# Two transformer blocks on one core: four projection stages with the weights as the 512-column moving operand

## The reference

```
q, f, i, o_gate, pool_v, gate_a, gate_b = split(x @ w_in)
o = hgrn2(silu(q), 1 - f, i, log f)                    # 8 heads of 128
o = o * rsqrt(mean(o*o, per head) + eps)
o = o * norm_g * sigmoid(o_gate);  a = o @ w_a          # og
...
h = rmsnorm(x); q, k, v, gu, gv, ... = split(h @ w_in_2)
attention(rope(q), rope(k), v)                          # v2
z = spatial_gate(rmsnorm(gelu(gv)));  gelu(gu) * z      # gv
k, v = split(rmsnorm(mem) @ w_kv)                       # cross attention, xv
...
peer_ffn: top-16 of 128 x 128 expert keys per head, rows of w_down and w_up gathered
```

## Time and profile before

| what | value |
|---|---|
| median of 3 runs | 1317.92 us |
| profiled execution | 1317.83 us, its span 1315.7 us |
| busy share of the span | TensorE 91%, VectorE 70%, ScalarE 41%, GpSimd 21% |
| chain that ended last, by engine | TensorE 57%, DMA 31%, VectorE 4%, issue 3%, ScalarE 2% |
| granted TensorE clock, mean | 0.983 of full speed |

### The profile page before, as it was taken

One profiled execution on the slowest core, in us unless ns is written; L12 is line 12 of the kernel. 1 busy time (PEld: TensorE's weight loads), 2 busy tenths in 40 slices (PEclk: granted clock), 3 DMA queues, 4 the chain that ended last, 5 costly groups with the idle time before them and its releaser, 6 DMA issues.

```text
span 1315.7 us, 17013 instructions
## 1 busy us (share of the span) xinstructions
PE 1196.4 (91%) x6094; PEld 855.7 (65%) x6094; DVE 923.9 (70%) x1841; ACT 543.2 (41%) x976; POOL 282.7 (21%) x261
## 2 busy tenths in 40 slices
PE   9999999999999999999999999999877877877776
PEld 9999999888888999998865445444322323323322
DVE  6885667887854775557788777676777777777655
ACT  5843454566633536536643333223322132232312
POOL 0000000000000000000044445444644344534420
PEclk9999999999999999999999999999999899989999
DMA  7543455545565644456699999999999999999996
GB/s 284 192 171 118 161 189 206 182 164 188 192 224 192 212 174 160 161 180 249 260 393 419 420 419 420 420 419 419 420 420 419 420 420 420 421 419 421 419 420 255
DMA packets 55926, 396.69 MB, mean 302 GB/s; under 512 B 6320, under 2 KB 6320, under 8 KB 8624
## 3 DMA queue, kind: packets, MB, share of 16 engines
q0 software_dynamic: 36864, 268.45, 49.3%
q1 hardware_dynamic: 17136, 119.16, 25.5%
q10 hardware_dynamic: 1856, 8.13, 1.8%
HBM read 394.67 MB, written 1.05 MB: 301 GB/s over the span
## 4 chain that ended last, share of the span: by engine, by line
PE 57%; DMA 31%; DVE 4%; issue 3%; ACT 2%; POOL 1%; DVEq 0%; POOLq 0%; ACTq 0%
DMA R<-experts,IDX 31%; PE ps L594 21%; PE ps L677 10%; PE ps L1154 8%; PE ps L891 4%; PE ps L606 3%; PE ps L893 2%; PE ps L644 2%; POOL R L2724 1%; PE ps L1006 1%; DVE R L2510 1%; PE ps L1033 1%; ACT DIAG L1591 1%; PE ps L1060 1%; PE ps L715 1%
## 5 line engine op out<-in xcount | busy, mean ns | idle before, releaser
L1154 PE MATMUL ps<-R,DIAG 128*128 128x512 f32 x1020 | 484.9, 623 | 103.8 <-ACT DIAG L1591 99.4
L1154 PEld LDWEIGHTS ps<-R,DIAG 128*128 128x128 f32 x1020 | 191.5, 197 | 372.4 <-issue 204.6
L2510 DVE CUSTOM_DVE_ANT_0 R<-R,XN 128x1024 f32<-128x1024 f32 x256 | 313.6, 1227 | 144.0 <-DMA R<-experts,IDX 141.2
L2724 POOL DMA_INDIRECT R<-experts,IDX x256 | 281.4, 1099 | 541.1 <-PE ps L1154 281.5
L1722 DVE TENSOR_TENSOR w_lo<-raw,w_hi 128x1024 fp32r<-128x1024 f32 x204 | 241.8, 1220 | 79.2 <-ACT w_hi L1207 75.4
L1207 ACT ACTIVATE w_hi<-raw 128x1024 fp32r<-128x1024 f32 x203 | 204.7, 1051 | 78.3 <-DMA raw<-weights 78.2
L1579 ACT ACTIVATE act_d<-dots,rst 128x2 f32<-128x2 f32 (+1 forms) x130 | 38.5, 296 | 330.6 <-DVE dots L2510 330.6
L1591 ACT ACTIVATE DIAG<-con,coef 128x128 f32<-128x128 f32 x255 | 88.6, 394 | 121.5 <-DVE coef L2519 113.1
L594 PE MATMUL ps<-opA_lo,w_hi 128*128 128x256 f32 x384 | 109.5, 285 | 0.4 <-issue 0.4
L594 PE MATMUL ps<-opA_hi,w_hi 128*128 128x256 f32 x384 | 108.6, 283 | 0.0
L594 PE MATMUL ps<-opA_hi,w_lo 128*128 128x256 f32 x384 | 108.6, 283 | 0.0
(11 more groups left out here) (401 smaller groups left out, 1706.7 us busy)
## 6 DMA issues: line engine op xcount, KB each, us to landing
raw<-weights SPq DMA_DIRECT2D x103, 1024.0 KB, 4.8
PQW<-weights SPq DMA_DIRECT2D x6, 1024.0 KB, 8.7
R<-experts,IDX POOLq DMA_INDIRECT x256, 31.8
LNR<-rows ACTq DMA_DIRECT2D x3, 1024.0 KB, 5.0
raw<-weights SPq DMA_DIRECT2D x4, 512.0 KB, 8.3
XF<-xT SPq DMA_DIRECT2D x2, 512.0 KB, 5.6
MEM<-mem ACTq DMA_DIRECT2D x1, 1024.0 KB, 5.2
XR<-x ACTq DMA_DIRECT2D x1, 1024.0 KB, 7.8
```

Source lines behind the costliest of these rows:

```text
L1154: mm = pe.matmul(psum[:, 4 + 2 * m + n, :], DIAG[:, k, :], rows_[:, D + n * 512:D + (n + 1) * 512], start=(it % 8 == 0 and k == 0), stop=True,
L2510: dve.tensor_tensor_reduce(out=rows_[:, 0:D], in0=rows_[:, 0:D], in1=XN[:, m, :], scale=1.0, scalar=0.0, op0=ALU.mult, op1=ALU.add, accum_ ...
L2724: pool.indirect_dma_start(out=R[u][:, :], out_offset=None, in_=experts, in_offset=bass.IndirectOffsetOnAxis(ap=IDX[:, it, k:k + 1], axis=0 ...
```

## The change

The four stages get their weights packed like those of `i` (two blocks are 512 output columns by 1024 inputs), 128 tokens of the activation stand, and 512 columns stream. A bank holds one half of the tokens by 512 columns and collects two blocks. The results of og have the tokens on the partitions now; the gate is multiplied before the transposes, and norm gain and split are done as the transposed rows are read.

```diff
+BY_ROWS = ("og", "xv", "v2", "gv")
-        OG = unit("OG", 22, [P, HEADS, T])
+        OG = unit("OG", 22, [P, MT, D])
         def group(eng, stage, j):
-            eng.wait_ge(gemm_done, group_end(stage, j))
+            if stage in BY_ROWS:
+                eng.wait_ge(gemm_done, half_end(BLOCK[stage] + j // 2 * 2 + 1, j % 2))
+            else:
+                eng.wait_ge(gemm_done, group_end(stage, j))
+            def by_rows(stage, g, k, op):
+                b = BLOCK[stage] + 2 * g + k
+                for m in range(MT):
+                    r = RING[stage] + 2 * g + m
+                    if k == 0:
+                        free_bank(r)
+                    for h in range(2):
+                        w = take(b % 4, half_end(b, h))
+                        for i in (2 * h, 2 * h + 1):
+                            for n, (a, o) in enumerate(parts(w, op)):
+                                mm = pe.matmul(bank(r), o[:, 4 * k + i, m * P:(m + 1) * P],
+                                               a[:, 2 * i:2 * i + 2, :].rearrange("p a b -> p (a b)"),
+                                               start=(k == 0 and i == 0 and n == 0),
+                                               stop=(k == 1 and i == 3 and n == 2), skip_group_check=True)
+                        if m:
+                            mm.then_inc(gemm_done, 1)
-            one("og", 0, opA, across)
+            by_rows("og", 0, 0, opA)
...
-                one("xv", j, opB, down)
+                by_rows("xv", 0, j, opB)
...
+            def evac_rows(stage, j, dst, func, further=True):
+                pb = group(act, stage, j)
+                drain(act.activation(dst, pb, func), stage, j)
+                if further:
+                    ahead(BLOCK[stage] + j + 3)
-                evac("og", j, OG[:, 2 * j:2 * j + 2, :], ACT.Sigmoid)
+                evac_rows("og", j, OG[:, j % 2, 512 * (j // 2):512 * (j // 2) + 512], ACT.Sigmoid)
...
-                if j == 2:
+                if j == 1:
                     for g in range(4):
                         act.wait_ge(pooled_ready, g + 1)
                         hi_of(g, PV[:, 2 * g:2 * g + 2, :], opB)
+                if j >= 2:
+                    hi_turned("oT", 2 * j - 4, opC, "hg")
+                    hi_turned("oT", 2 * j - 3, opC, "hg")
...
-                if j == 0:
-                    for g in range(4):
-                        act.wait_ge(o_ready, g + 1)
-                        hi_of(g, OG[:, 2 * g:2 * g + 2, :], opC)
-            evac("xv", 0, VX[:, :, 0:256], ACT.Copy, further=False)
+            evac_rows("xv", 0, VX[:, 0, :], ACT.Copy, further=False)
...
+            wait_stage(dve, "og", 4)
+            for m in range(MT):
+                st.do(dve.tensor_tensor(OG[:, m, :], psum[:, 4 + 2 * m:6 + 2 * m, :].rearrange("p a d -> p (a d)"),
+                                        OG[:, m, :], ALU.mult))
             ahead_low(23)
...
-            normed(0)
-            normed(1)
             for g in range(4):
                 lo_of(g, PV[:, 2 * g:2 * g + 2, :], opB, "pooled")
             ahead_low(25)
-            normed(2)
-            normed(3)
+            lo_turned("o", "oT", 0, opC, "hg")
+            lo_turned("o", "oT", 1, opC, "hg")
             ahead_low(26)
-            for j in range(4):
-                lo_of(j, OG[:, 2 * j:2 * j + 2, :], opC, "o")
+            lo_turned("o", "oT", 2, opC, "hg")
+            lo_turned("o", "oT", 3, opC, "hg")
```

More of the change, by code:

```diff
@@ L821, in _ @@
             keys_turn(1)
-            one("og", 0, opA, across)
+            by_rows("og", 0, 0, opA)
             cross(0)
             cross(1)
-            one("og", 1, opA, across)
+            by_rows("og", 0, 1, opA)
             state(0)
             state(1)
-            one("og", 2, opA, across)
+            by_rows("og", 1, 0, opA)
             cross(2)
             cross(3)
-            one("og", 3, opA, across)
+            by_rows("og", 1, 1, opA)
             outputs(0)
@@ L919, in _ @@
             for j in range(2):
-                one("v2", j, opC, down)
+                by_rows("v2", 0, j, opC)
             def att_scores(a):
@@ L976, in _ @@
             att_turn(0)
-            one("gv", 0, opC, down)
+            by_rows("gv", 0, 0, opC)
             att_scores(1)
-            one("gv", 1, opC, down)
+            by_rows("gv", 0, 1, opC)
             att_values(0)
@@ L1393, in _ @@
             scaled(1)
-            evac("xv", 1, VX[:, :, 256:512], ACT.Copy, further=False)
+            evac_rows("xv", 1, VX[:, 1, :], ACT.Copy, further=False)
             ahead(BLOCK["q2"])
@@ L1403, in _ @@
             for j in range(2):
-                evac("v2", j, V2[:, :, 256 * j:256 * j + 256], ACT.Copy)
+                evac_rows("v2", j, V2[:, j, :], ACT.Copy)
             def exps(a):
@@ L1427, in _ @@
             for j in range(2):
-                evac("gv", j, GV[:, :, 256 * j:256 * j + 256], ACT.Gelu_apprx_tanh)
+                evac_rows("gv", j, GV[:, j, :], ACT.Gelu_apprx_tanh)
             exps(1)
@@ L1948, in _ @@
                 ins = dve.tensor_tensor(
-                    ON[:, m], psum[:, 4 + 2 * m:6 + 2 * m, :].rearrange("p a (h d) -> p (a h) d", d=P),
+                    ON[:, m], OG[:, m, :].rearrange("p (h d) -> p h d", d=P),
                     st16[:, HEADS * m:HEADS * m + HEADS].rearrange("p (h d) -> p h d", d=1)
@@ L2753 @@
     pieces = [
-        k1024(f_), k1024(q_), wide(i_), k1024(pv_), k1024(og_), k1024(ga_), k1024(gb_),
+        k1024(f_), k1024(q_), wide(i_), k1024(pv_), wide(og_), k1024(ga_), k1024(gb_),
         a["w_pool"][0].reshape(4, 2, P, 256).transpose(2, 0, 1, 3).reshape(1, P, 2048),
@@ L2758 @@
         wide(a["w_down"][0]),
-        k1024(a["xa_w_kv_2"][0][:, 512:]), k1024(a["xa_w_kv_2"][0][:, 256:512]),
-        k1024(w2[:, 0:512][:, order]), k1024(w2[:, 512:1024][:, order]), k1024(w2[:, 1024:1536]),
-        k1024(w2[:, 1536:2048]), k1024(w2[:, 2048:2560]), k1024(w2[:, 2560:3584]),
+        wide(a["xa_w_kv_2"][0][:, 512:]), k1024(a["xa_w_kv_2"][0][:, 256:512]),
+        k1024(w2[:, 0:512][:, order]), k1024(w2[:, 512:1024][:, order]), wide(w2[:, 1024:1536]),
+        k1024(w2[:, 1536:2048]), wide(w2[:, 2048:2560]), k1024(w2[:, 2560:3584]),
         k1024(w2[:, 3584:4608]), k512(a["moba_w_proj_2"][0]), k512(a["gmlp_w_proj_2"][0]),
```

## The result

The changed kernel takes 1319.03 us (median of 20 runs, 1316.89 to 1321.08) against 1317.47 before (20 runs beside them): ratio 1.0014, 95% interval 1.0008 to 1.0020. It saves matmul time and is 1 to 2.6 us slower, within what was called no change (0.2%, 2.6 us). Its profiled execution took 1317.42 with a span of 1315.7, the same span as in the trace of before. All medians and ratios in this document are of undisturbed runs; five runs of 1525 to 3026 us, four of the kernel before and one of the kernel with split matmuls, are left out.

The account below looks back on a forecast made before the run. TensorE was taken to bound the front, whose gains or losses shift the tail one for one. og -1.24, xv +1.05, v2 and gv +1.25 sum to +1.1 us on 1317.83: forecast 1318.9, range 1315.2 to 1321.2.

Parts of the forecast that it names:

- base of 1317.83: Time of the profiled execution of the kernel before, span 1315.7 and 2.1 around it, to which the forecast's sum was added.
- 3.1 less 4.2: Whole forecast: 3.1 us saved in matmuls, 4.2 given back in waits.
- Matmuls, 0.31 a block: Four stages: a block takes 5.45 us instead of 5.76, over ten blocks 3.1 us saved.
- The rival that nothing is saved: Third rival: longer matmuls save nothing in the four stages, block 5.70 to 5.76, time 1321.4; chance 0.05.
- og, -1.24 and no stall: Stage og, four blocks: 1.24 us gained; transposes reusing the banks covered by 0.7, so no wait of TensorE.
- xv, +1.05: Stage xv, two blocks: late first eviction makes TensorE wait for scaled rows and q2's low parts, net 1.05 us lost.
- v2 and gv, +1.25: Stages v2 and gv, four blocks: late attention weights and second GV eviction, TensorE resumes at 535.85 instead of 534.59.
- Sum +1.06: Total of og, xv, and v2 with gv: -1.24 + 1.05 + 1.25, given there as +1.1 us.
- pure shift: Tail after the first indices: moves as a whole, one for one with the front, nothing else changing.
- halfway forms: Waits hidden at one pair only: 1316.5 to 1317.8 us; chance 0.10.
- first rival: The waits at the late evictions are hidden and the 3.1 us comes whole: 1314.7; all hidden, chance 0.07.
- delays of 3.2 and 2.6 against slacks of 3.5 and 2.0: TensorE's head start of 0.6 us adds to each delay: 3.2 in xv's pair, 2.6 at v2's attention weights.

Follow-up runs that it names:

- kernel with split matmuls: The change with each 512-column matmul of the four stages issued as two of 256, same banks, signals and order: 1321.53 us against 1318.00 before, ratio 1.0023.
- reordered kernels: The change with ScalarE's order altered in three places, ratio to before 0.9977; the same with ga2's third block's split also ahead of GV's evictions, 0.9962.
- first timing: The change against the kernel before: 1319.03 us against 1317.47, ratio 1.0014.
- the second: The unaltered change timed once more against the kernel before: 1318.39 us against 1318.00, ratio 1.0002 (0.9993 to 1.0011).

## Why the prediction was right

Forecast 1318.9, measured 1319.03. That these lie 0.1 apart is luck in part: the forecast stood on a base of 1317.83 where the runs beside the change gave 1317.47, and it added 1.06 where the timing rose by 1.56. What was right is the mechanism, saving less waits: 3.1 less 4.2 was forecast, 2.9 less 4.2 is what the table and the chains give. By its steps:

- *Matmuls, 0.31 a block*: 0.28 in og; 0.32 in xv, where the reordered kernels show the pair at 10.88 against 11.51. The stage "i" was the right row to take the price from; the kernel with split matmuls shows that it is the instruction's length and not the new order that saves. The rival that nothing is saved is refuted here. With it goes the use of the gap formula of the Trainium skill ("TensorE: Matmul & The Clock Gate", section "Back-to-back issue gap"): the page gives it for an isolated matmul, and for this stream it would make, as an estimate, 0.06 a block.
- *og, -1.24 and no stall*: -1.14 and none; the transposes came at 171.23, 0.9 behind the low parts, where 0.7 was forecast. ScalarE's turned batches ended at 168.6, forecast 168.5; VectorE's low parts at 170.35, forecast 170.4.

```profile
167.03 1.55 ACT L1284 ACTIVATE both_C<-ps,vec 128x256 fp32r<-128x256 f32 x4
168.49 1.86 DVE L1737 SCALAR_TENSOR_TENSOR both_C<-ps,vec,both_C 128x256 fp32r<-128x256 f32 x4
```

- *xv, +1.05*: +1.05. Waits 0.4 and 0.9, forecast 0.3 and 0.9. What carried the step is that the slack of 3.5 us was compared with the delay and the head start of TensorE together: a faster TensorE comes earlier to the place where it waits.
- *v2 and gv, +1.25*: +1.34. The weights of attention came 25.4 after v2's start, forecast 25.5; the waits were 1.1 for them and 1.3 for GA, forecast 1.2 and 1.4.
- *Sum +1.06*: +1.25 by the three stretches and +1.4 and +1.6 by the fronts in the traces at one pace, +1.56 in the first timing, +0.4 in the second.

Three things were not right. The text took the span of one execution of before as a fixed base; its up stage had the slower pace, and a comparison of the two profiled spans (1315.7 and 1315.7) would have shown no loss at all, as the pace hides 1.6 to 1.7 of it. The tail was taken as a pure shift: span less first gather is 659.2 and 659.3 in the two traces of before, 659.5 and 658.5 in the two of the change. So a microsecond of it moves by itself. And the halfway forms of the first rival are given as 1316.5 to 1317.8, where the forecast's own terms make 1316.4 (v2 and gv covered) and 1317.2 (xv covered).

The price of the moved signals was worked out in the forecast and not its remedy: that 1.36 us of earlier signal was all that the change lacked stood in the same numbers (delays of 3.2 and 2.6 against slacks of 3.5 and 2.0).

## What to carry to other kernels

Before a result is gathered over more work in one buffer, ask when its first signal comes and what is queued behind the instruction that waits for it: here 3 us saved by longer matmuls came with 4 us of waits, none of them for the results themselves. Signal each buffer when it is complete, and put work that does not need it ahead of its eviction: here either of these turned a front 1.4 to 1.6 longer into one 2.4 to 2.8 shorter. And when a microsecond matters, compare traces stage by stage with a second trace of the same kernel beside them.

## What the runs showed of the hardware

The matmuls of the stage up go in pairs, one of 512 columns on the high part of a piece of weights and one of 256 on its low part, 16 pairs a block. They run at one of two paces, constant over the 16 blocks of an execution: 5.547 or 5.653 us a block, a difference of 0.107, or 6.7 ns a pair. 3 of 13 traces have the slower one, and one kernel shows both. The granted clock is 1.00 in that stretch in both. The stage down behind it, 512 columns alone, takes 87.05 and 87.08 in two such executions. What sets the pace was not found and not looked for further; ten traces at the faster pace and three at the slower do not tell whether a kernel's code, or the chip, shifts the odds.
